# Gate vectors as rows through DRAM instead of broadcast matrix products in a two-layer hybrid trunk

## The reference, cut to what matters

```
c_act = silu(c)
for l in range(2):
    mod = c_act @ ada_w[l] + ada_b[l]
    sh_a, sc_a, gt_a, sh_m, sc_m, gt_m = split(mod, 6)
    h = rms_norm(x, norm_mix) * (1 + sc_a) + sh_a
    o = mixers(h @ w_in)               # MLA, forgetting and sparse attention
    x = x + gt_a * (o @ w_out)
    h = rms_norm(x, norm_mlp) * (1 + sc_m) + sh_m
    u = square(relu(h @ mlp_w1))       # width 8192
    x = x + gt_m * (u @ mlp_w2)
out = rms_norm(x, final_norm)
```

## Time and profile before

| what | us |
|---|---|
| three timed runs, median (lowest to highest) | 2434.97 (2433.05 to 2437.22) |
| the profiled execution, its own time | 2436.38 |
| span from its first to its last instruction | 2434.5 |
| PE busy in the span | 2327.7 |
| DVE busy | 1718.7 |
| ACT busy | 1139.3 |

### The profile page before, as it was taken

The page is one execution under the profiler, slowest core; times in us unless marked ns, Lnnn a source line. Parts: engine busy times, 40 slices in busy tenths (PEclk is TensorE's granted clock), DMA queues, the critical chain, the costliest instruction groups (busy, mean ns, idle before and its releaser), DMA issues.

```text
span 2434.5 us, 29301 instructions
## 1 busy us (share of the span) xinstructions
PE 2327.7 (96%) x11145; PEld 1912.0 (79%) x11145; DVE 1718.7 (71%) x2094; ACT 1139.3 (47%) x1584; POOL 19.2 (1%) x52
## 2 busy tenths in 40 slices
PE   3798999999999999999999999999999999999998
PEld 2686778778888888888878777888788888888887
DVE  7985788889787787887767667786666555555455
ACT  3253355545534434434446445454553453443453
POOL 1000000000000000000000000000000000000000
PEclk9799999999999999999999999999999999999999
DMA  9979986889889899898878798466677666666653
GB/s 367 384 257 337 332 283 204 270 295 329 286 303 313 298 329 321 299 327 300 299 239 273 252 319 279 152 217 208 211 258 239 183 188 196 185 189 191 190 186 126
DMA packets 318611, 633.90 MB, mean 260 GB/s; under 512 B 20428, under 2 KB 41352, under 8 KB 317832
## 3 DMA queue, kind: packets, MB, share of 16 engines
q1 hardware_dynamic: 314432, 625.49, 76.8%
q10 hardware_dynamic: 4040, 6.54, 0.8%
HBM read 629.85 MB, written 2.10 MB: 260 GB/s over the span
## 4 chain that ended last, share of the span: by engine, by line
PE 82%; DVE 7%; DMA 5%; ACT 2%; issue 2%; SPq 1%; POOL 0%; ACTq 0%; POOLq 0%; DVEq 0%
PE acc L1740 18%; PE acc L1742 17%; PE acc L1741 17%; PE pair L1740 7%; PE pair L1742 7%; PE pair L1741 7%; DVE ada_acc L1183 3%; DMA w_raw<-in_w_in 2%; DMA arena<-in_ada_w 2%; DVE w_lo L1256 2%; PE bank_T L1600 1%; PE acc L1764 1%; PE pair L1791 1%; PE bank_O L1600 1%; ACT w_hi L774 1%
## 5 line engine op out<-in xcount | busy, mean ns | idle before, releaser
L1256 DVE TENSOR_TENSOR w_lo<-w_raw,w_hi 128x1024 fp32r<-128x1024 f32 (+3 forms) x764 | 906.4, 1190 | 399.0 <-ACT w_hi L774 397.6
L774 ACT ACTIVATE w_hi<-w_raw 128x1024 fp32r<-128x1024 f32 (+3 forms) x764 | 785.4, 1031 | 755.2 <-PE acc L1742 437.1
L1740 PE MATMUL acc<-w_hi,hT_hi 128*128 128x512 f32 (+3 forms) x1536 | 611.6, 398 | 28.9 <-DVE w_lo L1256 12.4
L1742 PE MATMUL acc<-w_lo,hT_hi 128*128 128x512 f32 (+3 forms) x1536 | 590.6, 385 | 0.0
L1741 PE MATMUL acc<-w_hi,hT_lo 128*128 128x512 f32 (+3 forms) x1536 | 590.0, 384 | 0.0
L1183 DVE SCALAR_TENSOR_TENSOR ada_acc<-w_raw,silu_c,ada_acc 128x1024 f32<-128x1024 f32 x300 | 383.5, 1278 | 1.1 <-DVE small L1336 0.4
L1740 PEld LDWEIGHTS acc<-w_hi,hT_hi 128*128 128x128 f32 x1536 | 292.1, 190 | 101.2 <-DVE w_lo L1256 21.9
L1742 PEld LDWEIGHTS acc<-w_lo,hT_hi 128*128 128x128 f32 x1536 | 291.9, 190 | 56.3
L1741 PEld LDWEIGHTS acc<-w_hi,hT_lo 128*128 128x128 f32 x1536 | 292.7, 191 | 51.2 <-issue 1.7
L1740 PE MATMUL acc<-w_hi,uT_hi 128*128 128x512 f32 (+1 forms) x656 | 257.0, 392 | 0.0
L1742 PE MATMUL acc<-w_lo,uT_hi 128*128 128x512 f32 (+1 forms) x656 | 254.7, 388 | 0.0
(11 more groups left out here) (256 smaller groups left out, 1927.2 us busy)
## 6 DMA issues: line engine op xcount, KB each, us to landing
w_raw<-in_mlp_w SPq DMA_DIRECT2D x512, 512.0 KB, 4.8
w_raw<-in_ada_w SPq DMA_DIRECT2D x320, 512.0 KB, 5.7
w_raw<-in_w_in SPq DMA_DIRECT2D x112, 512.0 KB, 5.3
arena<-in_ada_w SPq DMA_DIRECT2D x64, 512.0 KB, 11.2
w_raw<-in_w_out SPq DMA_DIRECT2D x64, 512.0 KB, 5.6
w_raw<-in_nsa_cmp_k_w SPq DMA_DIRECT2D x32, 512.0 KB, 6.7
w_raw<-in_nsa_cmp_v_w SPq DMA_DIRECT2D x32, 512.0 KB, 6.4
w_raw<-in_w_in SPq DMA_DIRECT2D x16, 388.0 KB, 5.3
```

The source lines that it names most:

```text
L774: a.activation(w_hi[:, at % RING, :, 0:n], w_raw[:, i % RAW, :, 0:n], ACT.Copy).then_inc(hi_done, 1)
L1256: v.tensor_tensor(w_lo[:, at % RING, :, 0:n], w_raw[:, RING_NO["lo", Q] % RAW, :, 0:n], w_hi[:, at % RING, :, 0:n].bitcast(F32), ALU.subtr ...
L1740: pe.matmul(o, st_hi[:, kt + k, tok], wh, start=first and k == 0, stop=False)
L1742: mm = pe.matmul(o, st_hi[:, kt + k, tok], wl, start=False, stop=last and k == 1)
```

## The change

The gate vectors are no longer made as columns or by products with 128 columns of ones. After the 16 tiles of a G or H block, one T step `rowG0`, `rowG1`, `rowH0` or `rowH1` makes four float32 products. Each multiplies 32 columns of ones with 256 columns of `ada_acc` and writes 32 partitions of `bank_T`, a quarter of the array for each: the 1024 sums of the block now lie as four rows of 256. DVE adds them (128x256) to a small buffer `gate_sum`, into which four DMAs (32 partitions of 1 KB each) have put the bias row. ACT then issues a DMA of four rows to a DRAM tensor (`gate_out`, 4 KB), and some pieces later one that brings the 1024 values back to all partitions (`gate_in`, 512 KB, into `GTA` or `GTM`). The residual waits for this DMA.

Taken out are the second T step of each G block, `gta0` to `gta3`, `gtm0` to `gtm3`, the diagonals and the 1 MB bias DMA. The H1 block of layer 0 is moved from pieces M+34 to M+52 to M+31 to M+46, one tile for each piece, and that of layer 1 ends at M+44 instead of M+51. Two residuals of layer 0 stand three pieces later. Two waits are added that order DVE's buffers: the slot of head 4 waits for the first `gate_out`, and the rotary step of `uq0` and `uq1` waits for DVE's own `vc` step.

```diff
-             (126, "onsa0"), (127, "onsa1"), (128, "onsa2"), (129, "onsa3"), (132, "gta0"), (133, "gta1"),
-             (138, "gta2"), (139, "gta3"), (142, "ofox0"), (143, "ofox1")]
+             (126, "onsa0"), (127, "onsa1"), (128, "onsa2"), (129, "onsa3"), (142, "ofox0"), (143, "ofox1")]
...
-        block_at(0, "G", 0, 58, 85, "adaG0")
-        block_at(0, "G", 1, 91, 113, "adaG1")
+        block_at(0, "G", 0, 58, 85, "rowG0")
+        block_at(0, "G", 1, 91, 113, "rowG1")
...
-        block_at(1, "H", 0, F + 118, F + 142, None)
-        steps += [(146, "gtm0"), (147, "gtm1")]
+        block_at(1, "H", 0, F + 118, F + 142, "rowH0")
...
-    side(F + 143, ("bias", l), 4)
-    for j in range(4):
-        side(F + (130 if j < 2 else 136), ("diag", l, j), 5)
+    for b, q in ((0, 66 if l == 0 else 20), (1, 106)):
+        side(F + q, ("gate_bias", l, "G", b), 5)
+    for b, q in ((0, 89 if l == 0 else 34), (1, 117)):
+        side(F + q, ("gate_out", l, "G", b), 5)
+        side(F + 124 + b, ("gate_in", l, "G", b), 5)
+    for b, q in ((0, 8 if l == 0 else -14), (1, 10)):
+        side(M + q, ("gate_bias", l, "H", b), 5)
...
-        blocks.append((0, "H", 0, 12, 28, None))
-        mlp_steps += [(29, "gtm0", 0), (30, "gtm1", 0)]
-    blocks.append((l, "H", 1, 34 if l == 0 else 12, 53, None))
-    mlp_steps += [(54, "gtm2", 0), (55, "gtm3", 1)]
+        blocks.append((0, "H", 0, 12, 28, "rowH0"))
+    blocks.append((l, "H", 1, 31 if l == 0 else 12, 46, "rowH1"))
+    for b in range(2):
+        out_at = 50 if b else 32 if l == 0 else -12
+        side(M + out_at, ("gate_out", l, "H", b), 5)
+        side(M + out_at + (3 if l == 0 or b else 16), ("gate_in", l, "H", b), 5)
...
-                side(q, ("resid", l, (s, 4 + j), j), 3)
+                side(q + (3 if (l, s) == (0, 0) and j >= 2 else 0), ("resid", l, (s, 4 + j), j), 3)
...
+            def bias_gate(l, kind, b):
+
+                if kind == "H":
+                    act.wait_ge(s_pv, unit(l, UNIT_NO["fox", 3]))
+                at = (2 if kind == "G" else 5) * D + 1024 * b
+                for t in range(4):
+                    act.dma_start(gate_sum[kind, b][32 * t:32 * t + 32],
+                                  ada_b[l:l + 1, at + 256 * t:at + 256 * t + 256].broadcast_to([32, 256])
+                                  ).then_inc(gate_bias[kind, b], 16)
...
+            def send_gate(l, kind, b):
+
+                act.wait_ge(*t_is_free(l, f"row{kind}{b}"))
+                act.dma_start(gate_row(l, kind, b).rearrange("(t n) -> t n", t=4), gate_sum[kind, b][0:P:32, :]
+                              ).then_inc(gate_sent[kind, b], 16)
+
+            def fetch_gate(l, kind, b):
+
+                act.wait_ge(gate_sent[kind, b], 16 * l + 16)
+                if kind == "G":
+                    act.wait_ge(s_scores, unit(l, UNIT_NO["win", 6]))
+                else:
+                    act.wait_ge(s_pv, unit(l, UNIT_NO["fox", 3]))
+                to = (GTA if kind == "G" else GTM)[:, 1024 * b:1024 * b + 1024]
+                row = gate_row(l, kind, b).rearrange("(a n) -> a n", a=1)
+                act.dma_start(to, row.broadcast_to([P, 1024])).then_inc(gate_landed[kind, b], 16)
...
-                dve.wait_ge(*t_is_free(l, name))
+                dve.wait_ge(gate_landed["G" if type(chunk) is str else "H", j // 2], 16 * l + 16)
...
-                elif name[:3] == "gtm":
-                    j = int(name[3])
-                    gate = GTM[:, 512 * j:512 * j + 512]
+                elif name[:3] == "row":
+                    stage = gate_sum[name[3], int(name[4])]
                     dve.wait_ge(*t_is_full(l, name))
-                    dve.wait_ge(bias_landed, 16 * l + 16)
-                    v.tensor_tensor(gate, gate, FLAT[T_BANK[l, name]], ALU.add).then_inc(t_free[T_BANK[l, name]], 1)
+                    dve.wait_ge(gate_bias[name[3], int(name[4])], 64 * l + 64)
+                    v.tensor_tensor(stage, stage, FLAT[0][:, 0:256], ALU.add).then_inc(t_free[0], 1)
...
-                    elif name[:3] == "gta":
-                        j = int(name[3])
-                        pe.wait_ge(diag_done, 4 * l + j + 1)
-                        mm = pe.matmul(flat_, ones[:], ybuf[:, 1, j % 2, :], start=True, stop=True)
-                    elif name[:3] == "gtm":
-                        half = int(name[3]) % 2
+                    elif name[:3] == "row":
                         pe.wait_ge(ada_used, KT * ada_of(l, name) + KT)
-                        mm = pe.matmul(flat_, ones[:], ada_acc[:, 512 * half:512 * half + 512], start=True, stop=True)
+                        for t in range(4):
+                            mm = pe.matmul(flat_[32 * t:32 * t + 32, 0:256], ones[:, 0:32],
+                                           ada_acc[:, 256 * t:256 * t + 256], start=True, stop=True)
```

## The result

| | us |
|---|---|
| changed kernel, median of the timed runs (lowest to highest) | 2417.78 (2416.07 to 2422.52) |
| ratio to the kernel before, 95% interval | 0.9931 (0.9913 to 0.9948) |
| profiled execution, its own time and its span | 2416.07, 2414.2 |

The ratio is 16.8 us of 2435 (13 to 21). The forecast was 2420, with a range of 2414 to 2429.

What follows compares the result with a forecast made beforehand. PE was taken to bound the kernel (busy 96% of the span, 82% of the chain), with DVE or loads limiting in places. The terms summed to -14.9 us, from the median of 2434.97 to 2420, range 2414 to 2429.

Steps and rivals of the forecast that it cites:

- G1 of layer 0: Layer 0, block G1: transposes go, a row step comes, PE's lacking 0.78 us is won; -1.3 us (bounds -0.5 and -2).
- Gate products and diagonals of layer 0: Layer 0, `gta0` to `gta3` and diagonals: 3.44 us of PE and 1.57 of DVE go; -5.0 us.
- H of layer 0: Layer 0, H0 and H1: gate products go, row steps come, H0 also wins PE's lacking 0.69; -1.8 and -1.1 us.
- the dense block: Layer 0, H1 with one tile for each piece over 16 pieces: its denser loads cost +1.0 us (bounds 0 and 5.6).
- G blocks of layer 1: Layer 1, both G blocks: a row step replaces the transposes, 2 x (0.88 - 0.6); -0.6 us.
- Layer 1, F+118 to M+4: Layer 1: `gta` products and diagonals go, -4.9 us; H0's gate products go, within -2.2 for H0 and H1.
- my signs of being wrong: PE waits for `w_lo`, residuals waiting for a broadcast, ACT waits at store or DVE's add with PE idle, PE idle growing elsewhere.
- Broadcasts: Both layers, G broadcasts at F+124 and F+125: between 0 and 5.6 us, most fitting the free DMA share; +1.0 us.
- the quarters don't run in turn: Rival at all eight row steps: the quarters run one after another, 9.0 us worse, 2429; chance 0.05.
- the loads took nothing: Rival: G broadcasts and dense block cost 5.6 us each, 9.2 worse in sum, 2424 for one, 2429 both; chance 0.15.
- the gains of layer 0 passed through DVE's stretch: Rival in layer 0 after 507 us: loads set DVE's start, 6.3 us of G1 and `gta` lost, 2426; chance 0.08.
- no store stopped ACT: Rival: each of eight ACT stops at `gate_out` costs one piece, 22 us come, 14.9 go, 2442; chance 0.06.

## Why the prediction was right, step by step

- **What bounds it.** Right. The PE rows put in on their own moved their stages by their chain time, once the clock and the new wait are taken off: products by 3.5 and 3.4 for 3.4, row steps by 0.4 to 0.5 for 0.43. PE's share of the chain rose from 82 to 84%.
- **The row step.** 0.6 forecast, 0.57 measured, which is 3.0 times as fast as four products in turn (1.72). The Trainium skill, TensorE: Matmul & The Clock Gate, Part 3, gives 3.07 for four products packed by rows, from which I estimated 0.56. The trace agrees with that estimate, though these products are packed by columns, for which the Trainium skill has a figure for three tiles only (2.38).
- **G1 of layer 0.** -1.3 forecast, -1.6 in all nine executions that make G1 as a row once.
- **Gate products and diagonals of layer 0.** -5.0 forecast, -5.1 measured: 3.5 for the products and 1.4 to 1.5 for the diagonals. The bias DMA, which I had put at nothing, cost 0.9 to 1.7 when it was put back into the faster stage and nothing with the old gates, so the parts overlap and don't add up to the whole.
- **H of layer 0.** -1.8 and -1.1 forecast, -3.0 together, which is 2 x (1.72 - 0.57) + 0.69. That leaves nothing for the two residuals that were moved, which were not tried alone. The +1.0 for the dense block was not there.
- **G blocks of layer 1.** -0.6 forecast; G0 alone gave -1.4. PE's wait of 1.0 us ahead of those transposes, for DVE's step on the bank, went with them (the row below, of the kernel before, 1355 to 1366); I had not looked for it. G1's stage gave -2.2, of which 1.7 is a low clock of the kernel before that the changed kernel's execution did not meet.

```profile
PE bank_T L1647 <- DVE arena L1388: 1.0, 1, 1.0
```

- **Layer 1, F+118 to M+4.** -4.9 and -1.1 forecast, -5.5 measured. I gave the new wait on the bias rows no price; it costs 1.0 to 1.1, and the run with the later steps, at -6.6, shows it. DVE's add with PE idle behind it was one of my signs of being wrong, and this one came. That it cancels the 1.0 at G0 is luck.
- **H1 of layer 1.** -1.1 forecast, -1.0 measured.
- **Broadcasts.** +1.0 forecast, none measured. I had read the free DMA share at 420 to 430 (0.57), where they had landed already; in the windows in which they ran it was 0.73 and 0.66, and that was free enough.

The forecast sum was -14.9. On the profiles it is -20.3; without the low clock of before (1.7) and the front of layer 0 (0.6) it is -18.0, beside -16.8 (-21 to -13) on the timed runs. Of the 3.1 us between -14.9 and -18.0, 2.0 are what I had as costs (dense block, broadcasts) and the runs don't show; the rest is small terms. No rival came about: the quarters don't run in turn, the loads took nothing that the runs show of the 11.2 that I gave them as a rival, the gains of layer 0 passed through DVE's stretch (the products that begin it, at 505.80, now stand at 498.55, 7.3 us earlier, with the MLP 7.2 us earlier behind them), and no store stopped ACT long enough to be seen on PE.

## What to carry to other kernels

A product with 128 columns of ones makes the same column sums 128 times. With 32 columns of ones and four quarters of the output, a float32 sum of 1024 columns took 0.57 us where two full products took 1.72, and the copy to all partitions can go through DRAM, if the schedule has the time for it: the eight broadcasts took 4.6 to 7.3 us from issue to landing. Price such an edit by what the chain says each instruction adds, then look at every new wait for when its data is asked for, not only for how long its transfer takes. And compare two timelines piece by piece, with the granted clock and the waits of the engine beside them, before a difference of a few us in one stage is put down to an edit.

## What the runs showed that I had not expected

At PE's gap in the stage of layer 0 where DVE sets the pace, the granted clock fell in some executions and not in others. It was 1.00 in the kernel before, with a wait of 3.4 us, then down to 0.66 and 0.87 in two runs of the kernel with the diagonals back, with the same 3.4 us; 1.00 in the changed kernel and 0.83 in the one with later row steps, whose code is the same there, with 1.8 us. Each of these falls cost 1.4 to 3.0 us of PE's work, as much as most of the edits under study. What decides it stays open.
